# Hybrid diffusion step on one core: decayed keys before the last level's placement, turned keys read before the logarithm, three gate halves read in the next head's first level

## The chip, the cores and the metric

The kernel runs on one core of a Trainium2 chip. The metric is device time in microseconds (us) of one launch; the time before is the median of three runs. Engines are called as in the profile: PE is TensorE (PEld its weight loads), DVE VectorE, ACT ScalarE, POOL GpSimd, SP SyncE, which here only issues DMAs. Every engine runs its own instruction stream in the order in which it was written and waits on semaphores.

## What is computed

One trunk layer for 128 context tokens and 512 latent tokens (640 in all, width 1024): a mixer (a gated linear recurrence over four heads, called HGRN2, beside differential attention), then a mixture of 16 experts. The change lies in the recurrence alone:

```python
def hgrn2_scan(q, f, i, s0):              # f = forget gate, k = 1 - f, v = i, chunks of HG_CHUNK
    def step(S, inp):
        qc, lfc, kc, vc = inp             # lfc = log(f)
        b = jnp.cumsum(lfc, axis=2)
        inter = jnp.einsum('bhtd,bhde->bhte', qc * jnp.exp(b), S)
        rel = jnp.where(mask, b[:, :, :, None, :] - b[:, :, None, :, :], -jnp.inf)
        attn = jnp.einsum('bhtd,bhtsd,bhsd->bhts', qc, jnp.exp(rel), kc)
        o = inter + jnp.einsum('bhts,bhse->bhte', attn, vc)
        bL = b[:, :, -1]
        S = jnp.exp(bL)[..., None] * S + jnp.einsum('bhsd,bhse->bhde', kc * jnp.exp(bL[:, :, None] - b), vc)
        return S, o
# it runs forwards and backwards (own forget gates); o_f + o_b is RMS-normed per head and times silu(hg)
# the merge gates are g = sigmoid(h @ w_in[:, gate columns] + b_gate)
```

## The kernel before

One launch, all engines hand-scheduled: a list `STEPS` is written once, and each engine's program walks it and issues its own part of every step. So the place of a step in the list sets its place in the queue of every engine that has a part in it, and nothing else. PSUM is four pairs of banks; `use` books each write to a pair in the order of the list, `begin` makes PE wait until the pair's earlier contents were released, `filled` makes a reader wait for the writer.

Stages: norm and input projections (to about 204 us), attention with gate projections between (to 355), the recurrence of four heads (355 to 580), branch and output projections, router (to 740), experts (to the end). Projections in 32-bit are split into a high and a low part: three matmuls (lines 1750 to 1752) per tile, after ACT made the high part (`w_hi`, line 940) and DVE the low part (`w_lo`, line 1215).

A head `h` of the recurrence (the change is at its end and at the start of the next):

- **Levels** `("lev", h, 0..6)`: DVE subtracts (line 1299, always one level ahead), ACT takes two exponentials (line 1059), DVE makes two products (lines 1518, 1519), PE multiplies 20 small tiles (line 1953), DVE puts the scores of a level in their places (`place`: line 1307, for the last level 1311). Between the levels PE projects the next head's forget gates and queries (24 matmuls each).
- **`prep`**: ACT takes the exponentials `E[1]` (line 1069) and ten tiles of `exp(bL - b)` (line 1074, then `s_ebl2`), then copies the placed scores into `attn` (line 1078, then `s_attn`). DVE places level 5, then level 6, which waits for `s_attn`, then makes the **decayed keys** `Kb * E[0]` (line 1532), which PE waits for.
- **`kb`, `prep2`, `q`**: DVE makes the next head's `Kb` (1494) and `QB` (1538). ACT takes the next head's **logarithm** (line 1048, behind a table load of its own), DVE runs the two **scans** over it (1499, 1500). The scans stand ahead of `states` in DVE's queue.
- **`states`**: PE turns the decayed keys of both directions (line 1962), ACT reads them out of PSUM (**turned keys** `kTs`, the line 944 of 128x512), PE multiplies them with the values into `U` (1969), DVE reads `U` and carries the states `SC` (1547, 1553).
- **`qs`, `o`, `pre`, `diag`**: ACT's SiLU of the next queries (line 944, 128x640, with a table load); PE makes the head's output `o` (1979, 1984), which needs the last `SC`; DVE adds the keys (1506) and subtracts for level 0 (1299); PE makes the diagonal (1943), DVE reads it (1318).
- **Gate halves** `half(k, pair)`: 24 matmuls for half of a gate row; `drain(k)` is ACT's read of it (line 1098). Halves 25, 27 and 28 are made behind `states` of heads 0, 1, 2; half 26 behind `o` of head 0. SP stores them (line 792).
- **`sqr`**: ACT's square of `o` (1089), DVE's sum (1562), POOL's root (859, 860), DVE's two products (1568, 1571).

With heads 1 and 2 PE also makes a modulation row (`("mod", 7)`, `("mod", 8)`, 16 matmuls of line 1844) between the last level and the turns; ACT reads it behind the logarithm (`modr`).

Of the kernel before, what the change touches and what calls it, by code (L numbers as in the profile page):

```python
# [28 lines left out]
LEVELS = 7  # L29
# [10 lines left out]
def fused_step(nc, A, outs):  # L40
# [8 lines left out]
    with ExitStack() as ctx:  # L49
# [95 lines left out]
        kT = part(2560, 2560).rearrange("p (h t) -> p h t", h=H)  # L145
# [140 lines left out]
        STEPS = []  # L286
# [73 lines left out]
        def drain(k):  # L360
            STEPS.append(("glv", k // 2, k % 2))
# [29 lines left out]
        for h in range(H):  # L391
            todo = projections(h + 1) if h + 1 < H else []
            for lv in range(LEVELS):
                STEPS.append(("lev", h, lv))
                if (h, lv) in LEVEL_SPLITS:
                    split(*LEVEL_SPLITS[h, lv])
                if lv == 2 and h:
                    STEPS.append(("oTe", h - 1))
                if todo:
                    STEPS.append(todo.pop(0))  # L400
                if h + 1 < H and lv in (3, 5):
                    STEPS.append(("f", h + 1, lv // 2 - 1))
                if lv == 0:
                    if h == 0:
                        STEPS.append(("modr", 6))
                    if h == 1:
                        drain(26)
                    if h == 0:
                        STEPS.append(("modc", 6))
                    if h >= 2:  # L410
                        STEPS.append(("modv", 5 + h))
                    if h:
                        STEPS.append(("sqr", h - 1))
                if lv == 1 and h == 0:
                    STEPS.append(("modv", 6))
                if lv == 1 and h:
                    STEPS += [("sqg", h - 1), ("oT", h - 1)]
                if h == H - 1 and lv in (2, 4, 6):
                    drain(28 + lv // 2)
                if h == H - 1 and lv in (0, 2, 4):  # L420
                    half(29 + lv // 2, 1)
# [6 lines left out]
                STEPS.append(("kb", h + 1))  # L428
            STEPS.append(("prep2", h))
            if h + 1 < H:  # L430
                STEPS.append(("q", h + 1))
                if h == 0:
                    drain(24)
                else:
                    STEPS.append(("modr", 6 + h))
            else:
                STEPS.append(("hi", ("br", 1, 0)))
            STEPS.append(("states", h))
            if h + 1 < H:
                STEPS.append(("qs", h + 1))  # L440
                k = (25, 27, 28)[h]
                half(k, 3)
                drain(k)
            else:
                STEPS.append(("lo", ("br", 1, 0)))
                STEPS += [("ol", kt) for kt in range(4, 8)]
                STEPS.append(("hi", ("br", 0, 0)))
# [52 lines left out]
        for st in STEPS:  # L500
            k = st[0]
# [39 lines left out]
            elif k == "states":  # L541
                h = st[1]
# [95 lines left out]
        for key, _, _ in PIECES:  # L638
            k = key[0]
# [282 lines left out]
        def _(act):  # L922
# [38 lines left out]
            for n, st in enumerate(STEPS):  # L961
                k = st[0]
# [48 lines left out]
                elif k == "da":  # L1011
# [19 lines left out]
                    if n >= 2:  # L1031
                        h, i = ITER[n - 2]
                        oa_made(act, n - 2)
                        a.activation(oa[:, h, P * i:P * i + P], oaT, ACT.Copy, scale=subln8).then_inc(s_oa, 1)
                elif k == "f":
                    h, d = st[1], st[2]
# [8 lines left out]
                elif k == "q":  # L1045
                    h = st[1]
# [18 lines left out]
                elif k == "prep":  # L1065
# [11 lines left out]
                    for r in HALF:  # L1077
                        ins = a.activation(attn_c[r, :, r], within[r], ACT.Copy)
                    ins.then_inc(s_attn, 1)
                elif k == "states":  # L1080
                    h = st[1]
                    for d in range(2):
                        evac(kTs[:, d, 0:512], ("kT", h, d), src=bank(6 + d))
# [109 lines left out]
        def _(dve):  # L1193
# [10 lines left out]
            def own(sig):  # L1204
                count[sig.name] = count.get(sig.name, 0) + 1
                dve.wait_ge(sig, count[sig.name])
# [211 lines left out]
            for n, st in enumerate(STEPS):  # L1418
# [107 lines left out]
                elif k == "prep":  # L1526
                    h = st[1]

                    place(h, LEVELS - 2)
                    place(h, LEVELS - 1)  # L1530
                    dve.wait_ge(s_ebl2, h + 1)
                    v.tensor_tensor(E[0], Kb, E[0], ALU.mult).then_inc(s_ksb, 1)
                    own(s_ksb)
                elif k == "prep2":
                    h = st[1]
                    dve.wait_ge(s_eb, h + 1)
# [679 lines left out]
```

## Time and profile before

| | us |
|---|---|
| median of 3 runs (lowest, highest) | 1310.19 (1309.8, 1312.47) |
| the profiled execution | 1313.82 |
| its span, first to last instruction | 1312.0 |
| recurrence, four heads with the first one's projections | about 355 to 580 |
| of it the four head ends | about 404 to 424, 457 to 480, 512 to 532, 556 to 575 |

Busy shares over the whole span: PE 94%, DVE 76%, ACT 55%. A busy PE is not always a fast one: the granted clock has two levels in this trace, 1.00 (2.4 GHz) and 0.50 (1.2 GHz). Inside the recurrence PE waits in many short stretches, and each row of a timeline names in brackets how long the engine sat idle ahead of it and which instruction ended that. The rows of an engine's timeline stand in the order of its queue, so the row behind a waiting one waits with it.

### The profile page before, as it was taken

How to read it: one execution, taken by the hardware profiler on the slowest of the kernel's cores; microseconds unless marked ns; L12 is line 12 of the kernel's file. 1: busy time of each engine (PE TensorE's matmuls, PEld its weight loads, DVE VectorE, ACT ScalarE, POOL GpSimd, SP SyncE). 2: the span in 40 equal slices, each digit the busy share in tenths (PEclk: the TensorE clock that was granted, in tenths of full speed). 3: DMA queues.
4: the chain of work that ended last, by engine and by line, in shares of the span. 5: the costliest groups of instructions: out<-in, count | busy, mean ns of one | idle time of the engine just before them, and what ended most of it. 6: DMA issues, size and time to landing. Idle time of an engine off the chain costs nothing.

```text
span 1312.0 us, 18145 instructions
## 1 busy us (share of the span) xinstructions
PE 1235.7 (94%) x6817; PEld 915.1 (70%) x6817; DVE 995.6 (76%) x968; ACT 727.5 (55%) x769; POOL 341.1 (26%) x192
## 2 busy tenths in 40 slices
PE   7989999999998989779899899999999999999995
PEld 2667888888978876779776366666666666666663
DVE  3777425564267797878956889999999999999993
ACT  3322225555456758553312377777777777777771
POOL 1022001112000010100000002555656665555322
PEclk9989999999998989889998799999999999999998
DMA  8711521112331233044535499999999999999991
GB/s 311 260 54 53 191 78 55 56 48 66 98 108 48 70 92 127 25 172 172 194 142 204 158 402 401 393 392 385 391 384 390 383 388 385 390 383 390 394 361 31
DMA packets 111858, 296.06 MB, mean 226 GB/s; under 512 B 7092, under 2 KB 33076, under 8 KB 111800
## 3 DMA queue, kind: packets, MB, share of 16 engines
q1 hardware_dynamic: 108280, 284.25, 57.9%
q0 software_dynamic: 3520, 11.01, 3.6%
q8 instruction: 39, 0.64, 0.2%
q14 instruction: 19, 0.16, 0.0%
HBM read 278.47 MB, written 16.78 MB: 225 GB/s over the span
## 4 chain that ended last, share of the span: by engine, by line
PE 48%; DVE 2%; DMA 1%; ACT 1%; issue 0%; POOL 0%; DVEq 0%; ACTq 0%; POOLq 0%
PE ps L1750 15%; PE ps L1751 15%; PE ps L1752 15%; PE ps L1844 1%; PE ps L2071 1%; PE ps L2087 1%; DVE arena L1339 1%; PE ps L2033 0%; PE ps L2046 0%; DMA arena<-in_w_out_dram 0%; DMA arena<-xn_rows,arena 0%; ACT w_hi L940 0%; DVE arena L1594 0%; DVE arena L1590 0%; DVE w_lo L1215 0%
## 5 line engine op out<-in xcount | busy, mean ns | idle before, releaser
L1750 PE MATMUL ps<-w_hi,act_hi 128*80 128x512 f32 (+1 forms) x856 | 341.0, 398 | 10.1 <-DVE arena L1243 4.0
L1669 DVE TENSOR_TENSOR w_lo<-arena,w_hi 128x2048 fp32r<-128x2048 f32 x144 | 325.5, 2286 | 22.5 <-ACT w_hi L1169 17.6
L1751 PE MATMUL ps<-w_lo,act_hi 128*80 128x512 f32 (+1 forms) x856 | 337.5, 394 | 0.0
L1752 PE MATMUL ps<-w_hi,act_lo 128*80 128x512 f32 (+1 forms) x856 | 336.6, 393 | 0.0
L1169 ACT ACTIVATE w_hi<-arena 128x2048 fp32r<-128x2048 f32 x135 | 258.6, 1918 | 93.9 <-PE ps L1752 93.7
L1750 PE MATMUL ps<-act_hi,w_hi 128*128 128x320 f32 x576 | 185.3, 322 | 6.0 <-DVE w_lo L1215 3.0
L1750 PEld LDWEIGHTS ps<-w_hi,act_hi 128*80 128x80 f32 (+1 forms) x856 | 139.0, 162 | 71.8 <-DVE arena L1243 4.9
L1752 PEld LDWEIGHTS ps<-w_hi,act_lo 128*80 128x80 f32 (+1 forms) x856 | 138.9, 162 | 59.4 <-issue 0.7
L1751 PE MATMUL ps<-act_lo,w_hi 128*128 128x320 f32 x576 | 179.9, 312 | 0.0
L1752 PE MATMUL ps<-act_hi,w_lo 128*128 128x320 f32 x576 | 179.9, 312 | 0.0
L1751 PEld LDWEIGHTS ps<-w_lo,act_hi 128*80 128x80 f32 (+1 forms) x856 | 139.2, 163 | 55.4 <-issue 1.1
L859 POOL TENSOR_SCALAR arena<-arena 128x1 f32<-128x1 f32 (+2 forms) x44 | 13.8, 313 | 450.5 <-ACT arena L1025 190.3
L1750 PEld LDWEIGHTS ps<-act_hi,w_hi 128*128 128x128 f32 x576 | 110.3, 192 | 9.3 <-DVE w_lo L1215 3.6
L1215 DVE TENSOR_TENSOR w_lo<-arena,w_hi 128x2048 fp32r<-128x2048 f32 (+1 forms) x34 | 73.6, 2166 | 56.6 <-ACT w_hi L940 55.8
L1669 DVE TENSOR_TENSOR act_lo<-arena,act_hi 128x2048 fp32r<-128x2048 f32 x48 | 109.8, 2287 | 7.4 <-ACT act_hi L1169 6.1
L944 ACT ACTIVATE arena<-ps 128x512 f32<-128x512 f32 (+5 forms) x81 | 48.9, 616 | 117.3 <-PE ps L1844 32.2
L905 POOL DMA_INDIRECT out_dram<-arena x16 | 73.0, 4563 | 151.9 <-DVE arena L1695 151.9
L1751 PEld LDWEIGHTS ps<-act_lo,w_hi 128*128 128x128 f32 x576 | 110.2, 191 | 0.0
L1752 PEld LDWEIGHTS ps<-act_hi,w_lo 128*128 128x128 f32 x576 | 110.0, 191 | 0.0
L1169 ACT ACTIVATE act_hi<-arena 128x2048 fp32r<-128x2048 f32 x45 | 86.3, 1918 | 36.6 <-PE ps L1752 35.8
L940 ACT ACTIVATE w_hi<-arena 128x2048 fp32r<-128x2048 f32 (+1 forms) x34 | 61.5, 1810 | 54.8 <-PE ps L1752 25.9
L1844 PE MATMUL ps<-arena 128*2 128x512 f32 x144 | 71.5, 655 | 7.1 <-DMA arena<-in_w_mod_dram 7.1
(220 smaller groups left out, 1732.6 us busy)
## 6 DMA issues: line engine op xcount, KB each, us to landing
arena<-in_w_exp_gate_dram SPq DMA_DIRECT2D x64, 1024.0 KB, 8.5
arena<-in_w_exp_up_dram SPq DMA_DIRECT2D x64, 1024.0 KB, 7.0
arena<-in_w_exp_down_dram SPq DMA_DIRECT2D x64, 1024.0 KB, 7.9
arena<-in_w_mod_dram SPq DMA_DIRECT2D x23, 1024.0 KB, 5.2
arena<-in_w_in_dram SPq DMA_DIRECT2D x18, 1024.0 KB, 5.8
arena<-in_w_in_dram SPq DMA_DIRECT2D x12, 512.0 KB, 5.2
gl_raw<-arena SPq DMA_DIRECT2D x32, 160.0 KB, 1.8
arena<-gl_raw SPq DMA_DIRECT2D x8, 640.0 KB, 10.3
```

Of the source, the lines that this page charges most:

```text
L859: link(g.tensor_scalar(out, ss, 1.0 / n, EPS, ALU.mult, ALU.add))
L905: g.indirect_dma_start(out=y_sample[0], out_offset=bass.IndirectOffsetOnAxis(ap=iscat[0:CAP_LAT, 0:1], axis=0), in_=ye[0:CAP_LAT, :], in_o ...
L940: a.activation(hl(key)[0][:, 0:w], rawv(key)[:, 0:w], ACT.Copy).then_inc(s_hi, 1)
L944: release(a.activation(dst, src, func, **kw), key)
L1169: a.activation(EWh[j % NEW], eraw[(j + 2) % NRE], ACT.Copy).then_inc(s_eh, 1)
L1215: v.tensor_tensor(l_[:, 0:w], rawv(key)[:, 0:w], h_[:, 0:w].bitcast(F32), ALU.subtract).then_inc(s_lo, 1)
L1339: ins = v.scalar_tensor_tensor(out=out, in0=w[:, kk, :], scalar=by, in1=out, op0=ALU.mult, op1=ALU.add)
L1669: v.tensor_tensor(EWl[sl], eraw[slot], EWh[sl].bitcast(F32), ALU.subtract).then_inc(s_el, 1)
L1750: t.matmul(out, sh, mh, start=start, stop=False)
L1751: t.matmul(out, sh, ml, start=False, stop=False)
L1752: return t.matmul(out, sl, mh, start=False, stop=stop)
L1844: ins = t.matmul(bank(2 * modpair(j))[0:2, :], cond[:, kt, :], w[:, kk, :], start=kt == 0, stop=kt == 7)
```

## The change

Three moves and no new instruction:

1. In `prep` of every head DVE makes the decayed keys ahead of the placement of level 6. They wait for `s_ebl2` alone.
2. ACT's read of the turned keys becomes a step of its own, `("kT", h)`, ahead of the next head's logarithm in heads 0 to 2; in head 3 it stays behind the same weight split.
3. ACT's reads of gate halves 25, 27 and 28 go from behind their own matmuls into level 0 of the next head, behind its exponentials (and a weight split, where one stands there); that of half 26 goes behind the square of head 0's output.

```diff
@@ -401,16 +401,18 @@
                 if lv == 0:
+                    if h:
+                        drain((25, 27, 28)[h - 1])
                     if h == 0:
                         STEPS.append(("modr", 6))
-                    if h == 1:
-                        drain(26)
                     if h == 0:
                         STEPS.append(("modc", 6))
                     if h >= 2:
                         STEPS.append(("modv", 5 + h))
                     if h:
                         STEPS.append(("sqr", h - 1))
+                    if h == 1:
+                        drain(26)
@@ -428,19 +430,18 @@
             if h + 1 < H:
-                STEPS.append(("q", h + 1))
+                STEPS += [("kT", h), ("q", h + 1)]
                 if h == 0:
                     drain(24)
                 else:
                     STEPS.append(("modr", 6 + h))
             else:
-                STEPS.append(("hi", ("br", 1, 0)))
+                STEPS += [("hi", ("br", 1, 0)), ("kT", h)]
             STEPS.append(("states", h))
             if h + 1 < H:
                 STEPS.append(("qs", h + 1))
                 k = (25, 27, 28)[h]
                 half(k, 3)
-                drain(k)
@@ -1077,7 +1078,7 @@
-                elif k == "states":
+                elif k == "kT":
                     h = st[1]
                     for d in range(2):
                         evac(kTs[:, d, 0:512], ("kT", h, d), src=bank(6 + d))
@@ -1527,10 +1528,10 @@
                     place(h, LEVELS - 2)
-                    place(h, LEVELS - 1)
                     dve.wait_ge(s_ebl2, h + 1)
                     v.tensor_tensor(E[0], Kb, E[0], ALU.mult).then_inc(s_ksb, 1)
                     own(s_ksb)
+                    place(h, LEVELS - 1)
```

PE's, POOL's and SP's queues are the same instruction for instruction; only DVE's and ACT's differ.

ACT at the end of head 1, before. The 64x5x64 row is the last copy into `attn`, 1048 the logarithm with its table load, 2x512 the modulation row, 128x512 the turned keys, 128x640 the SiLU, 1098 the read of half 27, 1059 the next head's exponentials:

```order
L1078 ACTIVATE arena<-arena 64x5x64
L1048 ACT_TABLE_LOAD
L1048 ACTIVATE arena<-arena 128x1280 [waits s_f]
L944 ACTIVATE arena<-ps 2x512 [waits psum_full0]
L944 ACTIVATE arena<-ps 128x512 [waits psum_full3] x2
L944 ACT_TABLE_LOAD [waits psum_full1,s_qb]
L944 ACTIVATE arena<-ps 128x640
L1098 ACTIVATE arena<-ps,arena 128x320 [waits psum_full3,s_gst1]
L1059 ACT_TABLE_LOAD
L1059 ACTIVATE arena<-arena 128x2x5x64 [waits s_sub]
```

The same place in the changed kernel (its lines below the first edit are one or two higher):

```order
L1079 ACTIVATE arena<-arena 64x5x64
L945 ACTIVATE arena<-ps 128x512 [waits psum_full3] x2
L1049 ACT_TABLE_LOAD
L1049 ACTIVATE arena<-arena 128x1280 [waits s_f]
L945 ACTIVATE arena<-ps 2x512 [waits psum_full0]
L945 ACT_TABLE_LOAD [waits psum_full1,s_qb]
L945 ACTIVATE arena<-ps 128x640
L1060 ACT_TABLE_LOAD
L1060 ACTIVATE arena<-arena 128x2x5x64 [waits s_sub]
L1060 ACTIVATE arena<-arena 128x2x5x64
L941 ACTIVATE w_hi<-arena 128x2048 [waits psum_full3,s_raw1]
L1099 ACTIVATE arena<-ps,arena 128x320 [waits psum_full3,s_gst1]
```

The two reads that wait for PE's turns (`psum_full3`) now stand ahead of the logarithm and its table load, and the read of half 27 stands behind the exponentials and the split of a weight.

DVE at the same place, before: 1307 places level 5, 1311 level 6, 1532 is the decayed keys, 1494 the next `Kb`, 1538 `QB`, 1499 and 1500 the scans, 1547 the first read of `U`:

```order
L1307 COPY_PREDICATED arena<-arena,ps 128x320 [waits psum_full3,psum_free2]
L1311 COPY_PREDICATED arena<-arena,ps 64x5x64 [waits s_attn,psum_full2,psum_free3]
L1311 COPY_PREDICATED arena<-arena,ps 64x5x64
L1532 TENSOR_TENSOR arena<-arena 128x1280 [waits s_ebl2,psum_free2]
L1494 TENSOR_SCALAR arena<-arena 128x1280 [waits s_fa,s_ksb]
L1538 TENSOR_TENSOR arena<-arena 128x2x512 [waits s_st0,s_eb,s_f]
L1499 SCALAR_TENSOR_TENSOR arena<-arena 128x640 [waits s_ln,s_qb]
L1500 SCALAR_TENSOR_TENSOR arena<-arena 128x640 [waits s_v]
L1547 COPY arena<-ps 128x128 [waits psum_full2,s_st,s_scan]
```

And in the changed kernel:

```order
L1308 COPY_PREDICATED arena<-arena,ps 128x320 [waits psum_full3,psum_free2]
L1532 TENSOR_TENSOR arena<-arena 128x1280 [waits s_ebl2,psum_free3]
L1312 COPY_PREDICATED arena<-arena,ps 64x5x64 [waits s_attn,psum_full2,s_ksb]
L1312 COPY_PREDICATED arena<-arena,ps 64x5x64
L1495 TENSOR_SCALAR arena<-arena 128x1280 [waits s_fa,psum_free2]
L1539 TENSOR_TENSOR arena<-arena 128x2x512 [waits s_st0,s_eb,s_f]
L1500 SCALAR_TENSOR_TENSOR arena<-arena 128x640 [waits s_ln,s_qb]
L1501 SCALAR_TENSOR_TENSOR arena<-arena 128x640 [waits s_v]
L1548 COPY arena<-ps 128x128 [waits psum_full2,s_st,s_scan]
```

The decayed keys no longer wait for `s_attn`; the scans still wait for the logarithm (`s_ln`), and the reads of `U` still stand behind the scans.

ACT in level 0 of head 1, changed kernel: 1060 the exponentials of levels 0 and 1, 1099 the reads of halves 25 and 26, 1090 the square of head 0's output, which stood before in the order 25, exponentials, 26, square:

```order
L1060 ACTIVATE arena<-arena 128x2x5x64 [waits s_sub]
L1060 ACTIVATE arena<-arena 128x2x5x64
L1099 ACTIVATE arena<-ps,arena 128x320 [waits psum_full3,s_gst1]
L1090 ACTIVATE arena<-ps 128x640 [waits psum_full0,s_scan]
L1099 ACTIVATE arena<-ps,arena 128x320 [waits psum_full3,s_gst0]
L1060 ACTIVATE arena<-arena 128x2x10x32 [waits s_sub]
```

The exponentials of level 0 no longer stand behind half 25, and the square no longer behind half 26; those of level 1 stand behind half 26 as before.

## Rows read from the trace of the kernel before

**Rows 1.** ACT's timeline, end of head 0: start, length, instruction [idle before <-releaser].

```profile
419.79 0.53 ACT L1098 ACTIVATE arena<-ps,arena 128x320 f32<-128x320 f32 x1 [5.72 <-PE ps L1752]
```

**Rows 2.** DVE's timeline, end of head 0.

```profile
405.93 1.05 DVE L1311 COPY_PREDICATED arena<-arena,ps 64x320 f32<-64x320 uint8 x2 [1.71 <-ACT arena L1078]
...
410.77 1.49 DVE L1499 TENSOR_TENSOR_SCAN arena<-arena 128x640 f32<-128x640 f32 x1
...
423.09 0.82 DVE L1518 TENSOR_TENSOR arena<-arena 128x640 f32<-128x640 f32 x1 [2.17 <-ACT arena L1059]
```

**Rows 3.** PE's timeline, end of head 0 and level 1 of head 1.

```profile
411.71 3.75 PE L1969 MATMUL ps<-arena 128*128 128x128 f32 x16 [2.06 <-ACT arena L944]
...
419.51 0.61 PE L1979 MATMUL ps<-arena 128*128 128x128 f32 x4
...
432.48 0.74 PE L1953 MATMUL ps<-arena 128*64 128x64 f32 x18 [1.01 <-DVE arena L1519]
```

**Rows 4.** ACT's timeline, end of head 1.

```profile
462.43 1.27 ACT L1048 ACTIVATE arena<-arena 128x1280 f32<-128x1280 f32 x1 [2.28 <-DVE arena L1494]
464.61 1.61 ACT L944 ACTIVATE arena<-ps 2x512 f32<-2x512 f32 x3 [0.92 <-PE ps L1844]
466.24 1.28 ACT L944 ACT_TABLE_LOAD   x1
467.54 0.70 ACT L944 ACTIVATE arena<-ps 128x640 f32<-128x640 f32 x1
```

**Rows 5.** DVE's timeline, end of head 1 and level 0 of head 2.

```profile
463.80 1.49 DVE L1499 TENSOR_TENSOR_SCAN arena<-arena 128x640 f32<-128x640 f32 x1
...
467.14 0.29 DVE L1547 COPY arena<-ps 128x128 f32<-128x128 f32 x1 [0.33 <-PE ps L1969]
...
474.85 0.82 DVE L1518 TENSOR_TENSOR arena<-arena 128x640 f32<-128x640 f32 x1 [0.87 <-ACT arena L1059]
...
477.15 2.29 DVE L1215 TENSOR_TENSOR w_lo<-arena,w_hi 128x2048 fp32r<-128x2048 f32 x1
```

**Rows 6.** PE's timeline, end of head 1, levels 0 and 1 of head 2.

```profile
464.45 1.09 PE L1962 MATMUL ps<-arena 128*128 128x128 f32 x8
...
471.26 0.61 PE L1979 MATMUL ps<-arena 128*128 128x128 f32 x4
...
479.50 0.64 PE L1750 MATMUL ps<-act_hi,w_hi 128*128 128x320 f32 x1 [2.10 <-DVE w_lo L1215]
...
485.73 0.69 PE L1953 MATMUL ps<-arena 128*64 128x64 f32 x16
```

**Rows 7.** A stretch of 2 us: busy (x instructions) of PE, PEld, DVE, ACT, POOL, clock, DMA.

```profile
480.00:482.00 2.00, 2.00 (x9) 2.00 (x8) 1.93 (x3) 0.07 (x1) 1.49 (x1) 0.50 0.66 143
```

**Rows 8.** DVE's timeline, end of head 2 and level 0 of head 3.

```profile
518.15 1.49 DVE L1499 TENSOR_TENSOR_SCAN arena<-arena 128x640 f32<-128x640 f32 x1
...
522.01 0.29 DVE L1547 COPY arena<-ps 128x128 f32<-128x128 f32 x1 [0.83 <-PE ps L1969]
...
529.71 0.82 DVE L1518 TENSOR_TENSOR arena<-arena 128x640 f32<-128x640 f32 x1 [0.88 <-ACT arena L1059]
```

**Rows 9.** PE's timeline, end of head 2.

```profile
519.31 1.09 PE L1962 MATMUL ps<-arena 128*128 128x128 f32 x8
```

**Rows 10.** ACT's timeline, end of head 3.

```profile
555.84 3.02 ACT L1074 ACTIVATE arena<-arena 128x128 f32<-128x128 f32 x10
```

**Rows 11.** DVE's timeline, end of head 3.

```profile
559.83 1.04 DVE L1311 COPY_PREDICATED arena<-arena,ps 64x320 f32<-64x320 uint8 x2 [3.53 <-ACT arena L1078]
...
566.53 0.29 DVE L1547 COPY arena<-ps 128x128 f32<-128x128 f32 x1 [2.87 <-PE ps L1969]
```

**Rows 12.** PE's timeline, end of head 3.

```profile
562.45 1.97 PE L1962 MATMUL ps<-arena 128*128 128x128 f32 x8 [5.82 <-DVE arena L1532]
...
569.59 0.68 PE L1979 MATMUL ps<-arena 128*128 128x128 f32 x4 [1.94 <-DVE arena L1553]
...
573.65 0.71 PE L1984 MATMUL ps<-arena 128*128 128x128 f32 x4
```

## The prediction

> **What bounds the kernel now.** The views were read in this order: the page's busy shares and slices (PE 94% busy; the waits of PE lie in the recurrence, 404 to 580 us), then the timelines of ACT, DVE and PE around the four head ends, since every moved step stands there. What the reader is to see in them is which engine is late to whom.
>
> At the end of head 0 DVE idles 1.71 us until the copies into `attn` are done and only then makes the decayed keys [rows 2]; PE idles until it has them, and 2.06 us more until ACT has read the turned keys [rows 3]. ACT sits 5.72 us before gate half 25 [rows 1], and the next head's exponentials, which stand behind it, keep DVE idle for 2.17 us [rows 2].
>
> At the end of heads 1 and 2 it looks alike and is not. There PE is busy with a modulation row until it turns the keys, at 464.45 and 519.31, with no idle time ahead [rows 6, 9]. The decayed keys were ready long before. The logarithm and the scans run in that time: the logarithm from 462.43 [rows 4], the scans from 463.80 and 518.15 [rows 5, 8]. DVE then waits only 0.33 and 0.83 us for PE at its first read of `U`, and 0.87 and 0.88 us for the exponentials [rows 5, 8]. So DVE's chain is nearly as late as PE's: scans, states, keys, level 0.
>
> At the end of head 3 no logarithm follows. PE idles 5.82 us for the decayed keys [rows 12], DVE 3.53 us for `attn` ahead of them [rows 11].
>
> **The sum** is made against the profiled execution: 1313.82 us, of which 1312.0 are span. It lies 3.6 above the median of 1310.19, so I add the difference to the median.
>
> One length serves three places. From the start of the first scan to the first product of the next head's level 0, DVE needs 474.85 - 463.80 - 0.33 - 0.87 = 9.85 us of its own work [rows 5]; head 2 gives the same (529.71 - 518.15 - 0.83 - 0.88 = 9.85) [rows 8]. The two products take 1.75 more.
>
> **Heads 1 and 2: the turned keys ahead of the logarithm.** ACT now waits for PE's turns with the logarithm queued behind, and DVE's scans, `U` reads and all of level 0 behind that. Head 1: turns from 464.45, the first half is there about 0.6 later (half of 1.09, and one matmul's depth), ACT reads both by 466.2 (1.1 of the 1.61 for three reads), then the table load, 1.28, which used to lie in idle time and is now exposed, then the logarithm, 1.27 [rows 4, 6]. It ends at 468.8 and the scans start at 468.85 instead of 463.80. First product: 468.85 + 9.85 = 478.7 instead of 474.85, since the two old waits are swallowed. That is **3.85 late**. The same working for head 2, turns at 519.31: scans at 523.7, first product at 533.55 instead of 529.71, again **3.85 late** [rows 8, 9].
>
> What PE makes of it. `o` of head 1 could start at 471.26 [rows 6]; it needs the last `SC`, which DVE now has 4.6 later, about 474.85. PE idles 3.6 us. After idles of 2.06 and 2.10 us it ran slowly (16 matmuls in 3.75 us; 9 in 2 us at a granted clock of 0.50) [rows 3, 6, 7], so I take `o` at the slow clock, as in head 3: 569.59 to 574.36, 4.8 us [rows 12]. It ends at 479.65, the diagonal and the turned row at 480.8, just as the products are done (480.45). DVE reads the diagonal until 481.05 and makes the low part of the forget weights, 2.29 [rows 5]: PE's projection starts at 483.4, 3.9 after the old 479.50 [rows 6]. But the old one ran at the slow clock, 6.2 us until 485.73 [rows 6, 7]. The new one has only 1.8 us of idle time ahead and a busy stretch of 6.5 us before that; I take it at full clock, 3.8 us, to 487.2. DVE's level 1 products, 3.95 late, end at 487.75. PE's level 1 starts at 487.8: **+2.1** for head 1. From there each engine waits on the others in a ring (projection, sigmoid, exponentials, products), so nothing swallows it.
>
> Head 2 had no slow stretch there to give back, and head 3's level 0 is a chain of DVE, ACT and POOL that PE waits for: **+3.9**. Bounds for these two: 0.9 better at each if the logarithm were not late (the exponentials leave their place behind the gate half, 0.87 and 0.88), 4.6 worse at each if every delay of the scans reached PE.
>
> **Head 0.** No modulation row stands in PE's way. Decayed keys from 405.0, when ACT's ten exponentials end (0.97 before it could place level 6), ready at 406.5; PE turns them at 407.0, when its projection ends. ACT reads them until 408.75, load and logarithm until 411.35, scans from 411.45: 0.7 late against 410.77 [rows 2]. First product of head 1: 411.45 + 9.85 = 421.3 instead of 423.09, **1.8 early**, since the exponentials no longer wait for half 25 [rows 1, 2]. PE makes `U` and half 25 by 414, then idles 3.4 us for `SC` (417.45 instead of the old start of `o` at 419.51 [rows 3]), pays the slow clock, 4.8 instead of 3.0, and ends `o` where it did before. Half 26, level 0 and a projection follow back to back as before, until 431.4. Level 1's products are then ready (the square is no longer behind half 26), where PE waited 1.01 us [rows 3]: **-1.1**. Bound: if the clock stays up, `o` ends 1.8 earlier, the half 26 waits for ACT's read of half 25 until 421.8, and level 1 starts at 430.0, -2.4.
>
> **Head 3.** The decayed keys start when the ten exponentials end, 555.84 + 3.02 = 558.86, instead of 560.90 behind `attn` and the placement [rows 10, 11]. PE, ACT, `U` and DVE's reads (waiting 2.87 us for PE [rows 11]) all follow 2.0 earlier; the weight split on ACT ends at 561.63, in time. **-2.0**. SP's gate loads start when this head's `o` is done, so the branch stage shifts as a whole.
>
> **No cost:** the level 6 placement (1.05) goes between the decayed keys and `Kb`; DVE reaches the scans before the logarithm is done. The late reads of halves 27 and 28 free pair 3 for level 1, which comes 6 us later, and SP's stores behind them come ahead of loads that wait longer for other slots.
>
> Sum: -1.1 + 2.1 + 3.9 - 2.0 = **+2.9 us**, 1313.1.
>
> Of a table switch the rows show 1.28 us, and the next instruction 0.02 us behind it (466.24 + 1.28, then 467.54) [rows 4]. The Trainium skill (ScalarE: Activation LUTs, What ACT_TABLE_LOAD costs) adds a drain of 1.38 us to each switch, 2.66 in all; the load newly exposed in heads 1 and 2 would then cost 2.8 more together, 1315.9. The trace doesn't show that drain, so the sum does not have it.
>
> **Rivals.**
> - *The clock falls once more* in the 1.8 us before head 2's first projection. For: 2.06 and 2.10 us of idle time made PE slow [rows 3, 6]. Against: 1.8 is less, and behind a long busy stretch. It would run 2.5 us slower; 0.6 of that is hidden under DVE: +4.9, 1315.1.
> - *Head 0 gives its bound*, the clock staying up: +1.6, 1311.8. Against: 3.4 us is more than any wait that left the clock up.
> - *Faster:* the scans' delay does not decide, as if ACT could serve the logarithm in time; then only waits vanish: -2.4, -0.9, -0.9, -2.0 = -6.2, 1304.0. It decides only where the logarithm ends within about 1.2 us (0.33 + 0.87) of its old time; the rows give 5.05. For it: my 0.6 for the turns and the exposed load are read from one execution each. That the reads still stand where they stood is ruled out by the order.
>
> **Chances.** Forecast 42%, clock falls once more 27%, head 0's bound 17%, faster 9%, larger losses 5%. The forecast's own spread is about 1.3 either way (1311.8 to 1314.4). About 0.2%, 2.6 us, is what a measurement of this kernel can tell from no change; the forecast lies just above it, so it feeds two chances: slower 57%, within 0.2% 33%, faster 10%. The range leaves out most of the faster case and the largest losses: 1310.0 to 1316.4.
>
> **What would show it.** In the changed profile: ACT's logarithm behind its two reads, ending near 468.8 less head 0's 1.1; DVE's scans 4 to 5 us later at heads 1 and 2; a PE wait of about 3.5 us before `o` in heads 0, 1 and 2, with a clock of 0.50 behind it; head 3's wait for decayed keys down from 5.82 to 3.8. Wrong would make it: `o` of heads 1 and 2 without a wait, or a clock that stays at 1.00 through them.

## The result and the profile after

| | before | changed |
|---|---|---|
| median of 7 runs each (lowest to highest), us | 1310.19 (1309.65 to 1312.47) | 1316.24 (1315.05 to 1317.28) |
| profiled execution, us | 1313.82 | 1316.05 |
| its span, us | 1312.0 | 1314.3 |

The ratio of times is 1.0038 with a 95% interval of 1.0029 to 1.0048: the change costs 5.0 us (3.8 to 6.3), 0.4%. The forecast was 1313.1, with a sum of +2.9. The sign and the steps on ACT and DVE were right, two terms were too small. The median of 1316.24 lies only 0.2 us inside the upper end of the range (1316.4) and outside the forecast's own spread (1311.8 to 1314.4).

The whole span says little here (2.3 us), since the profiled execution of before lies 3.6 us above its median, and the changed kernel is already 1.5 us ahead of it before the first moved step. So I read stretches between fixed points of PE's stream: **A** from the last level of head 0 to the turns of head 1, **B** from there to the turns of head 2, **C** from there to level 5 of head 3 (its last but one), **D** from there to the turn of head 3's output. Each holds one head end. The changed kernel and all those below start A 0.3 to 2.3 us earlier than the kernel before does (401.12 against 402.65 for the change); nothing moved lies ahead of A, and this is in none of the sums. Most of it goes with PE's clock in the input stage. From 20 to 30 us the kernel before had 0.89 and the changed one 1.00 (columns as in [rows 7]):

```profile
20.00:30.00 10.00, 8.50 (x36) 3.37 (x35) 5.50 (x9) 4.58 (x6) 1.48 (x4) 0.89 0.93 344
...
20.00:30.00 10.00, 8.27 (x38) 3.40 (x37) 5.55 (x8) 4.57 (x6) 1.48 (x4) 1.00 0.93 345
```

Of the thirteen profiled executions of this document, the four with 0.86 to 0.89 there begin A at 402.30 to 402.65, the nine with 1.00 at 400.37 to 401.47.

| us | A | B | C | D | sum |
|---|---|---|---|---|---|
| before | 61.80 | 54.86 | 34.78 | 25.36 | |
| forecast of the difference | -1.1 | +2.1 | +3.9 | -2.0 | +2.9 |
| changed | 60.16 | 57.84 | 39.68 | 23.41 | |
| measured difference | -1.64 | +2.98 | +4.90 | -1.95 | +4.3 |

The +4.3 lies inside the interval of the paired runs.

**Head 1.** ACT's timeline of the changed kernel (start, length, instruction, idle before). It answers to [rows 4]:

```profile
461.98 1.09 ACT L945 ACTIVATE arena<-ps 128x512 f32<-128x512 f32 x2 [6.84 <-PE ps L1963]
463.08 1.28 ACT L1049 ACT_TABLE_LOAD   x1
464.37 1.27 ACT L1049 ACTIVATE arena<-arena 128x1280 f32<-128x1280 f32 x1
...
475.40 1.89 ACT L941 ACTIVATE w_hi<-arena 128x2048 fp32r<-128x2048 f32 x1
477.20 0.51 ACT L1099 ACTIVATE arena<-ps,arena 128x320 f32<-128x320 f32 x1
```

ACT idles 6.84 us until PE has turned the keys, and only then come the table load and the logarithm. DVE's timeline, to be held against [rows 5]:

```profile
465.75 1.49 DVE L1500 TENSOR_TENSOR_SCAN arena<-arena 128x640 f32<-128x640 f32 x1 [6.67 <-ACT arena L1049]
...
475.65 0.82 DVE L1519 TENSOR_TENSOR arena<-arena 128x640 f32<-128x640 f32 x1
...
477.95 2.29 DVE L1216 TENSOR_TENSOR w_lo<-arena,w_hi 128x2048 fp32r<-128x2048 f32 x1
```

The scans wait 6.67 us for the logarithm. PE turned the keys at 461.28 (first row below), so the scans start 4.47 us and the first product 14.37 us behind the turns. In the kernel before the product stood 474.85 - 464.45 = 10.40 behind them [rows 5, 6]: 3.97 late. PE's timeline, for [rows 6]:

```profile
461.28 1.09 PE L1963 MATMUL ps<-arena 128*128 128x128 f32 x8
...
471.86 0.68 PE L1980 MATMUL ps<-arena 128*128 128x128 f32 x4 [3.60 <-DVE arena L1554]
...
474.93 0.80 PE L1944 MATMUL ps<-arena 128*64 128x64 f32 x20
477.76 0.41 PE L1763 MATMUL ps<-arena 2*128 2x2 f32 x4 [2.03 <-ACT arena L1099]
478.10 0.80 PE L1954 MATMUL ps<-arena 128*64 128x64 f32 x20
480.30 0.64 PE L1751 MATMUL ps<-act_hi,w_hi 128*128 128x320 f32 x1 [1.40 <-DVE w_lo L1216]
...
485.54 0.80 PE L1954 MATMUL ps<-arena 128*64 128x64 f32 x20
```

Two things are to be seen. PE waits 3.60 us before `o` (471.86), as forecast, and yet `o` takes only 3.07 us. And there is a wait that I did not have: 2.03 us before the turned modulation row (line 1763), ended by ACT's read of gate half 27 at 477.20. Two stretches (columns as in [rows 7]; the second is head 2's `o`):

```profile
480.00:482.00 2.00, 1.70 (x6) 1.70 (x7) 1.93 (x4) 0.31 (x1) 0.72 (x1) 0.57 0.32 38
...
529.70:532.00 2.30, 2.30 (x11) 2.30 (x12) 2.23 (x3) 0.03 (x1) 0.00 (x0) 0.50 0.18 57
```

In head 1 the projection behind the waits begins at a clock of 0.57, in head 2 `o` runs at 0.50. Head 1's `o`, behind the same wait of 3.60 us, ran at 1.00.

**Head 2.** PE's timeline, then DVE's:

```profile
519.12 1.09 PE L1963 MATMUL ps<-arena 128*128 128x128 f32 x8
...
529.70 1.19 PE L1980 MATMUL ps<-arena 128*128 128x128 f32 x4 [3.60 <-DVE arena L1554]
...
535.24 0.80 PE L1944 MATMUL ps<-arena 128*64 128x64 f32 x20
...
541.30 0.80 PE L1954 MATMUL ps<-arena 128*64 128x64 f32 x20 [0.48 <-DVE arena L1520]
```

```profile
533.50 0.83 DVE L1519 TENSOR_TENSOR arena<-arena 128x640 f32<-128x640 f32 x1
...
536.19 0.49 DVE L1319 TENSOR_TENSOR arena<-ps,arena 128x320 f32<-128x320 f32 x1 [1.01 <-PE ps L1944]
```

The same wait of 3.60 us, and here `o` takes 5.54 us at the lower clock. The diagonal is late, and DVE, which was already 3.97 late (533.50 is 14.38 behind the turns at 519.12), loses 1.01 us more.

**Heads 0 and 3.** Head 0, PE and DVE, for [rows 3] and [rows 2]:

```profile
405.47 1.03 PE L1963 MATMUL ps<-arena 128*128 128x128 f32 x8
...
416.00 1.19 PE L1980 MATMUL ps<-arena 128*128 128x128 f32 x4 [3.61 <-DVE arena L1554]
...
420.42 0.80 PE L1944 MATMUL ps<-arena 128*64 128x64 f32 x20
```

```profile
409.88 1.49 DVE L1500 TENSOR_TENSOR_SCAN arena<-arena 128x640 f32<-128x640 f32 x1 [1.69 <-ACT arena L1049]
...
419.80 0.83 DVE L1519 TENSOR_TENSOR arena<-arena 128x640 f32<-128x640 f32 x1
```

Head 3, PE's turns, for [rows 12], where the same row had 5.82:

```profile
565.22 1.97 PE L1963 MATMUL ps<-arena 128*128 128x128 f32 x8 [3.88 <-DVE arena L1532]
```

### The profile page after: what moved, and what is told of

The parts are those of the page before. It is cut to its first block, busy times and chain, and to the rows that moved or that the text cites. A ratio compares the mean times of both kernels' runs of the same rounds, so it can differ in the third digit from the quotient of the medians.

```text
span 1314.3 us, 18145 instructions
## 1 busy us (share of the span) xinstructions
PE 1233.8 (94%) x6817; PEld 915.6 (70%) x6817; DVE 995.6 (76%) x968; ACT 727.4 (55%) x769; POOL 341.0 (26%) x192
## 4 chain that ended last, share of the span: by engine, by line
PE 48%; DVE 2%; DMA 1%; ACT 1%; issue 0%; POOL 0%; DVEq 0%; ACTq 0%; POOLq 0%
PE ps L1751 15%; PE ps L1752 15%; PE ps L1753 15%; PE ps L1845 1%; PE ps L2072 1%; PE ps L2088 1%; DVE arena L1340 1%; PE ps L2034 0%; PE ps L2047 0%; DMA arena<-in_w_out_dram 0%; DMA arena<-xn_rows,arena 0%; ACT w_hi L941 0%; DVE arena L1595 0%; DVE arena L1591 0%; DVE w_lo L1216 0%
## 5 line engine op out<-in xcount | busy, mean ns | idle before, releaser
L901 POOL COPY arena<-arena 64x1 uint32 (+1 forms) x16 | 88.2, 5512 | 13.3 <-DMA out_dram<-arena 13.3
```

The lines of the kernel that those rows point to most:

```text
L901: g.tensor_copy(iscat[0:CAP_LAT, 0:1], iS[0:CAP_LAT, bass.ds(e, 1)]).then_inc(s_icq, 1)
```

## The experiments

The theory: in heads 1 and 2 the logarithm, put behind ACT's reads of the turned keys, delays DVE's scans and all that is queued behind them; the two other moves are gains that this swallows. The rivals: the loss comes from the late reads of the gate halves, which hold a PSUM pair longer; or from the clock, which falls in the new wait before `o`. Differences in the table below are to before, in us; "sum" is over the stretches A to D of one profiled execution each, "by runs" is the ratio with its interval, times the median of before (1310.2 to 1312.4, depending on the runs it was compared with). Where the two differ by a us or two, the ratio counts: each sum rests on one execution, and all are taken against the same execution of before, which was itself slow in places (head 1's projection above all, see p_keys).

| kernel | A | B | C | D | sum | by runs |
|---|---|---|---|---|---|---|
| changed | -1.64 | +2.98 | +4.90 | -1.95 | +4.3 | +5.0 (3.8 to 6.3) |
| p_turned | +1.31 | +3.00 | +5.14 | +0.12 | +9.6 | +7.6 (5.9 to 9.3) |
| p_drains | -1.01 | -1.84 | -0.84 | -0.08 | -3.8 | -5.6 (-7.3 to -3.9) |
| p_keys | -3.28 | -0.98 | -0.01 | -2.36 | -6.6 | -4.6 (-6.3 to -2.8) |
| p_head0 | -0.41 | -0.61 | -0.84 | -1.94 | -3.8 | -6.3 (-8.4 to -4.2) |
| q_keysdrains | -1.54 | -2.89 | -0.82 | -2.02 | -7.3 | -7.7 (-9.4 to -5.9) |
| q_scanslate | -2.70 | +2.40 | +2.22 | -1.94 | 0.0 | +0.1 (-1.0 to +1.4) |
| q_filler | -2.62 | +3.43 | +3.98 | -1.95 | +2.8 | +3.4 (2.1 to 4.9) |
| q_drainsplit | -0.15 | +1.95 | +4.07 | -1.94 | +3.9 | +4.6 (2.9 to 6.2) |
| r_fill | -4.10 | -1.96 | -0.84 | -0.94 | -7.8 | -6.7 (-8.5 to -5.0) |
| r_split | -1.56 | -1.83 | -0.85 | -1.95 | -6.2 | -6.2 (-7.9 to -4.3) |
| r_both | -4.11 | -2.09 | -0.84 | -0.99 | -8.0 | -6.6 (-8.4 to -4.7) |

### One part alone

p_turned: the kernel before with only the turned keys read ahead of the logarithm.

```diff
-                STEPS.append(("q", h + 1))
+                STEPS += [("kT", h), ("q", h + 1)]
...
-                elif k == "states":
+                elif k == "kT":
```

> Of the change only the move of ACT's read of the turned keys ahead of the next head's logarithm; the decayed keys and the gate halves stay as before. Theory (the logarithm and the scans behind the turned keys are the loss): heads 1 and 2 lose 3.9 us each at the first product of the next head, part of it hidden in PE's stream, head 0 stays within 0.5, head 3 unchanged: 6 to 8 us slower than before, and the whole loss of the change and more. Rival A (the gate halves held back cost the time): within 1 us of before. Rival B (the slow clock behind PE's wait for the states is the loss, whoever causes the wait): as the theory, but with no more than 2 us of it outside the stretches of clock 0.50.

p_drains: only the late reads of the gate halves.

```diff
                 if lv == 0:
+                    if h:
+                        drain((25, 27, 28)[h - 1])
...
                 half(k, 3)
-                drain(k)
```

> Of the change only the later reads of the gate halves. Theory: the next head's exponentials come 2.2, 0.9 and 0.9 us earlier; PE gains about 1 in head 0 and 0.9 in heads 1 and 2: 2 to 3 us faster than before. Rival A (the gate halves held back cost the time, since the turned modulation row waits for the pair that half 27 holds): 3 us slower or more.

p_keys: only the decayed keys ahead of the last placement.

```diff
                     place(h, LEVELS - 2)
-                    place(h, LEVELS - 1)
                     dve.wait_ge(s_ebl2, h + 1)
...
                     own(s_ksb)
+                    place(h, LEVELS - 1)
```

> Of the change only the decayed keys ahead of the last placement. Theory: head 3 gains 2.0, head 0 0.9 (the logarithm waits for the next keys, which come 0.9 earlier), heads 1 and 2 nothing, since PE is busy with the modulation row: 2.5 to 3 us faster. Rival A says nothing of it. Rival B (clock): head 3 gains more than 2, since its slow stretch is shorter.

Measured: one part alone costs 7.6 us (a ratio of 1.0058, 1.0045 to 1.0071), the two others each gain (0.9957, 0.9944 to 0.9970; and 0.9965, 0.9952 to 0.9979). p_turned carries +3.0 and +5.1 in heads 1 and 2, as the whole change does (+3.0 and +4.9). In head 0, where no more than 0.5 was expected, it loses 1.31: a new wait of 1.98 us stands before `o`, and `o` behind it took 4.66 us instead of 2.99. So the first rival falls: the late reads alone do not lose anything, they gain 5.6. Both gains were larger than expected. p_drains gave 1.84 in head 1 where 0.9 was the wait for the exponentials, because the projection behind it was shorter as well (5.24 instead of 6.23 us). p_keys gave 3.28 in head 0. There PE waits 2.80 us before `U`, in one piece instead of in two (1.39 and 2.06), and in this execution the clock stayed up behind it:

```profile
408.76 2.02 PE L1969 MATMUL ps<-arena 128*128 128x128 f32 x16 [2.80 <-ACT arena L944]
```

The profiled execution of p_keys, 1304.35, is the fastest of its six (median 1307.80), so its -6.6 says more than the kernel usually gives. Its -0.98 in head 1 is no gain of the move, of which nothing was expected there. The projection starts 15.05 us behind the turns in both kernels, but took 5.25 us here and 6.23 in the profiled execution of before. So before was slow at this place, and about 1 us of every B in the table is that slow stretch and not the edit. Against p_keys, whose head 1 has the same waits, the change loses 57.84 - 53.88 = 3.96 us there.

### The change without the turned keys, and with them in head 0 alone

q_keysdrains is p_drains and p_keys together, that is the change without ("kT", h); p_head0 is the change with ("kT", h) ahead of the logarithm in head 0 alone.

```diff
-                STEPS += [("kT", h), ("q", h + 1)]
+                if h in (0,):
+                    STEPS.append(("kT", h))
+                STEPS.append(("q", h + 1))
...
+            if h not in (0,):
+                STEPS.append(("kT", h))
             STEPS.append(("states", h))
```

> The change, but in heads 1 and 2 the turned keys are read behind the logarithm and the modulation row, as before. Theory: the two losses go and 0.9 is won in each, head 0 and head 3 keep their 1.6 and 1.9: 5.3 us faster than before, 9 to 11 faster than the change. Rival A (gate halves): still 1 us or more slower than before. Rival B (clock): the waits of 3.6 us ahead of the outputs of heads 1 and 2 are gone and with them the slow stretches, as the theory.

> The change without its middle part: decayed keys first and gate halves late, but the turned keys read behind the logarithm in every head. Theory (the logarithm behind the turned keys is the whole loss): the gains of the two parts add, about 1 (gate halves) and 3 (keys) in head 0, 1.8 in head 1, 0.8 in head 2, 2.3 in head 3: 8 to 9.5 us faster than before. Rival (the two gains are one and the same wait counted twice): no more than 5.5 faster, as either part alone.

Measured: 1306.79 for p_head0 (0.9952, 0.9936 to 0.9968) and 1305.02 for q_keysdrains (0.9941, 0.9928 to 0.9955). Both beat both kernels. For q_keysdrains 8 to 9.5 had been expected; 7.7 (5.9 to 9.4) is a little less. From q_keysdrains to the changed kernel the stretches differ by -0.10, +5.87, +5.72 and +0.07: in these executions the move of the turned keys costs 5.8 us in each of heads 1 and 2, and nothing in heads 0 and 3. For head 0 that is because each of the two has a slow stretch of its own there (`U` 3.75 us in q_keysdrains, `o` 4.42 in the change). Where neither has one, in r_fill and q_filler below, A is 57.70 without the move and 59.18 with it: it costs 1.5 us there too. PE's rows of q_keysdrains in head 1 show what the 5.87 is made of:

```profile
474.22 0.41 PE L1763 MATMUL ps<-arena 2*128 2x2 f32 x4 [1.06 <-ACT arena L1099]
...
476.77 0.42 PE L1751 MATMUL ps<-act_hi,w_hi 128*128 128x320 f32 x1 [1.40 <-DVE w_lo L1216]
...
480.94 0.80 PE L1954 MATMUL ps<-arena 128*64 128x64 f32 x20 [0.40 <-DVE arena L1520]
```

The turns of this kernel are at 462.56, so the projection starts 14.21 us behind them, against 19.02 in the changed kernel: 4.81, which is the 3.97 of the scans and the 0.84 that the freed exponentials had given and that is swallowed. The other 1.07 is the length of the projection with what follows, 4.17 here and 5.24 there. In head 2 the same 4.8 and 0.9 for `o` at the lower clock make the 5.72 (q_filler, below, has head 2 without the slow `o`, at 4.80).

### The scans behind the states

q_scanslate is the change, but the scans stand behind DVE's reads of `U` and not ahead of them.

```diff
             if h + 1 < H:
+                STEPS.append(("scan", h + 1))
                 STEPS.append(("qs", h + 1))
...
-                elif k == "q":
+                elif k == "scan" or k == "q" and st[1] == 0:
```

> The change, with DVE's two scans moved behind its reads of U and its states, so that only the next head's level 0 waits for the logarithm and no longer the states. Theory: PE's waits of 3.6 us ahead of the outputs of heads 0, 1 and 2 go to 0; the first product of the next head stands 12.3 us after the turns of heads 1 and 2 (before 10.4, with the change 14.4): heads 1 and 2 together lose 2 to 4 us against before instead of 7.9, so 4 to 6 us faster than the change. Rival (the loss is ACT's own, its exposed table load and logarithm in front of the exponentials): the first product stays at 14.4 and the time within 1 us of the change.

DVE's timeline in head 1, where PE turns the keys at 460.55:

```profile
463.25 0.29 DVE L1549 COPY arena<-ps 128x128 f32<-128x128 f32 x1 [4.90 <-PE ps L1971]
...
466.20 1.49 DVE L1501 TENSOR_TENSOR_SCAN arena<-arena 128x640 f32<-128x640 f32 x1
...
473.16 0.83 DVE L1520 TENSOR_TENSOR arena<-arena 128x640 f32<-128x640 f32 x1
```

Measured: 1311.97, no different from before (1.0001, 0.9992 to 1.0011), 5 us better than the change. All three waits before `o` are gone. The states fill the time in which DVE waited for the logarithm, and the first product stands 12.61 us behind the turns, between the 10.40 of before and the 14.37 of the change. So the loss is the place of the scans in DVE's queue together with the late logarithm, as the theory has it: the same table load and the same logarithm on ACT at the same place, with other work ahead of the scans, cost 2.2 instead of 4.0. What is left of the loss in B and C (+2.40, +2.22) is that product, 2.21 late. One wait in head 1 even grew, that before the turned modulation row:

```profile
475.27 0.58 PE L1764 MATMUL ps<-arena 2*128 2x2 f32 x4 [4.11 <-ACT arena L1100]
```

It did not cost time by itself: the projection behind it starts 2.21 us later than before, as the product does.

### Products in the wait before `o`

q_filler puts 12 products of the identity with itself, whose results nobody reads, ahead of `o` of heads 0 to 2.

```diff
+                    if h + 1 < H:
+                        for _ in range(12):
+                            t.matmul(bank(6)[:, 0:P], ident, ident, start=True, stop=True)
                     begin(pe, ("o", h))
```

> The change, with 12 matmuls of the identity with itself (results unused, into a free half of pair 3) ahead of the output of heads 0, 1 and 2, so that PE works through about 3.0 of the 3.6 us that it waits there. Clock theory: the outputs of heads 0 and 2, 4.4 and 5.5 us long with the change, take 3.0; head 2 gets 1 us shorter, head 0 up to 1.4: 2 to 3 us faster than the change. Rival (the clock costs nothing, DVE's chain decides): within 0.5 us of the change.

PE in head 1 (each of the twelve counts as two rows, x24):

```profile
466.80 2.84 PE L1977 MATMUL ps<-arena 128*128 128x128 f32 x24
470.57 0.68 PE L1983 MATMUL ps<-arena 128*128 128x128 f32 x4 [0.93 <-DVE arena L1554]
...
473.64 0.80 PE L1944 MATMUL ps<-arena 128*64 128x64 f32 x20
476.48 0.55 PE L1763 MATMUL ps<-arena 2*128 2x2 f32 x4 [2.04 <-ACT arena L1099]
```

Measured: 1315.09 (1.0026, 1.0016 to 1.0037), about 1.5 us less than the change, where 2 to 3 were expected; the two intervals overlap. In the trace the waits before `o` are down to 0.92 or 0.93 and `o` takes 3.07 us in all three heads; without the products it took that in one of nine cases (they are listed at the end). Head 0 gains 0.98 by that and head 2 gains 0.92, down to +3.98, which is DVE's lateness and nothing else. Head 1, whose `o` had not been slow, gains nothing and is even 0.45 longer: the 2.04 before the turned row stands, and the projection runs slowly behind it (5.67 us to level 1). So the clock is a second, smaller part: about 0.9 us in head 2. The second rival does not carry the loss.

### The half's read ahead of the weight split

q_drainsplit is the change, but ACT reads the gate half straight behind the first exponentials of the level, ahead of the split `w_hi`.

```diff
                 STEPS.append(("lev", h, lv))
+                if lv == 0 and h:
+                    drain((25, 27, 28)[h - 1])
                 if (h, lv) in LEVEL_SPLITS:
...
                 if lv == 0:
-                    if h:
-                        drain((25, 27, 28)[h - 1])
```

> The change, with ACT's read of gate halves 25, 27 and 28 ahead of the weight split of level 0 instead of behind it (differs in head 2's level 0 alone). Theory: the turned modulation row, which shares the bank of half 27, no longer waits 2.03 us, PE's projection behind it runs at full clock, and the stretch from the turns of head 1 to those of head 2 is 0.9 us shorter than with the change, 56.9 instead of 57.8; the split comes 0.5 later and must not be late. Rival (the wait is hidden, since the projection waits for the split weights anyway, and the clock falls all the same): 57.8 or 0.5 more.

PE and ACT in head 1 (turns at 463.96):

```profile
474.55 1.19 PE L1980 MATMUL ps<-arena 128*128 128x128 f32 x4 [3.61 <-DVE arena L1554]
...
479.19 0.80 PE L1944 MATMUL ps<-arena 128*64 128x64 f32 x20
480.25 0.80 PE L1954 MATMUL ps<-arena 128*64 128x64 f32 x20
483.01 0.41 PE L1751 MATMUL ps<-act_hi,w_hi 128*128 128x320 f32 x1 [1.95 <-DVE w_lo L1216]
```

```profile
478.08 0.51 ACT L1099 ACTIVATE arena<-ps,arena 128x320 f32<-128x320 f32 x1
478.50 1.90 ACT L941 ACTIVATE w_hi<-arena 128x2048 fp32r<-128x2048 f32 x1
```

Measured: the wait before the turned row is gone and B is 56.81, +1.95 where the change has +2.98. This `o` took 4.64 us, close to the 4.8 of the forecast, the projection stood behind 1.95 us of waiting (the forecast: 1.8) and ran at the full clock (4.18 us to level 1). That is the course that the forecast drew for head 1, and it gives the +2.1 of the forecast. The kernel as a whole, 1316.86 (1.0035, 1.0022 to 1.0047), is not told apart from the change. In the profiled execution `o` of head 0 took 5.81 us instead of 4.42 and gave the gain back; whether that holds for the others is not shown.

### Versions without the turned keys

r_fill is q_keysdrains with ten such idle products between the turns and `U` of head 0; r_split is q_keysdrains with the half's read ahead of the split; r_both has both.

```diff
+                    if h == 0:
+                        for _ in range(10):
+                            t.matmul(bank(5)[:, 0:P], ident, ident, start=True, stop=True)
                     for d in range(2):
```

> Decayed keys first and gate halves late, turned keys behind the logarithm as before; besides, 10 matmuls of the identity with itself (results unused, into a bank that U writes next) between the turns and U of head 0, where PE waits 2.8 us for ACT. Clock theory: U and gate half 25 always run at full clock, 5.4 us from U to the output instead of 8.2; the stretch from the last level of head 0 to the turns of head 1 is 57.5 us instead of 60.3 (before 61.8): 9 to 10 us faster than before. Rival (the clock is not the cause of the 8.2 us, DVE's chain is): 60 us, and about 7.5 faster.

> Decayed keys first and gate halves late, turned keys behind the logarithm, and the gate halves read ahead of the weight split of level 0. Theory: the turned modulation row of head 1 no longer waits the 1.06 us, but PE had slack there; within 0.5 us of the kernel with the split first, 7 to 8 us faster than before. Rival (this wait costs as it did in the changed kernel): 1 us faster than that.

> Both: the 10 matmuls in head 0 and the gate halves ahead of the split. Theory: 9 to 10 us faster than before, as with the matmuls alone. Rival: 7.5.

Head 0 of q_keysdrains, then of r_fill:

```profile
410.50 3.75 PE L1970 MATMUL ps<-arena 128*128 128x128 f32 x16 [2.81 <-ACT arena L945]
```

```profile
406.22 2.40 PE L1968 MATMUL ps<-arena 128*128 128x128 f32 x20
409.21 2.02 PE L1973 MATMUL ps<-arena 128*128 128x128 f32 x16 [0.59 <-ACT arena L945]
```

Measured: 1303.96 (0.9949, 0.9935 to 0.9962), 1305.67 (0.9953, 0.9940 to 0.9967) and 1303.68 (0.9950, 0.9936 to 0.9964). All are 6 to 7 us faster than before, and not told apart from each other or from q_keysdrains by these runs. For r_fill and r_both 9 to 10 had been expected, so by the whole time that expectation missed. In the trace the idle products do what they should: `U` takes 2.02 us instead of 3.75 and A falls by 2.56. One execution alone would not show that, since `U` took 2.02 in p_keys as well, behind the same wait without any product in it; but r_both has 2.02 too, and r_split, without the products, 3.75. But D is 1.08 longer than in q_keysdrains at places that nothing touched, and B 0.93 (the projection of head 1, 5.11 us instead of 4.17). In D it is the projection behind the same wait, first q_keysdrains, then r_fill:

```profile
567.60 0.42 PE L1751 MATMUL ps<-act_hi,w_hi 128*128 128x320 f32 x1 [2.41 <-DVE act_lo L1577]
```

```profile
564.84 0.64 PE L1751 MATMUL ps<-act_hi,w_hi 128*128 128x320 f32 x1 [2.41 <-DVE act_lo L1577]
```

0.42 and 0.64 for the same first matmul behind the same 2.41 us: one execution had the upper clock in the 3 us from there (1.00) and the other the lower (0.50). r_split saves nothing. Its wait of 1.06 us before the turned row is gone, but PE then waits 2.11 instead of 1.40 us for `w_lo` and its projection starts 14.21 us behind the turns (462.60), exactly as in q_keysdrains:

```profile
476.81 0.42 PE L1751 MATMUL ps<-act_hi,w_hi 128*128 128x320 f32 x1 [2.11 <-DVE w_lo L1216]
...
482.05 0.80 PE L1954 MATMUL ps<-arena 128*64 128x64 f32 x20
```

That its B is 1.06 longer (-1.83 against -2.89) is the length of this projection, 5.24 us instead of 4.17, and not the moved read. q_keysdrains is the only one of these kernels whose projection took 4.17; p_drains, with the same waits, took 5.24 as well.

## Why the prediction was right or wrong

- **The length of DVE's work** (9.85 us from the first scan to the first product): right. 475.65 - 465.75 = 9.90 in head 1, 9.92 in heads 0 and 2.
- **The late logarithm** of heads 1 and 2: right. The scans were forecast 4.40 us behind the turns and came 4.47 behind them; the product was forecast 3.85 late and came 3.97 late. That the load lies exposed at 1.28 us and no more is seen too: it starts at 463.08, and the logarithm at 464.37. The drain of 1.38 us that the Trainium skill (ScalarE: Activation LUTs, What ACT_TABLE_LOAD costs) adds to each switch is not in this trace. That the 1315.9 with this drain comes so near to the time measured is luck.
- **The wait before `o`**: right, 3.60 to 3.61 us in three heads, where 3.4 to 3.6 was forecast.
- **`o` at the slow clock, 4.8 us**: this term was mis-sized, both ways. It took 4.42, 3.07 and 5.54 us behind the same wait. The price came from the one slow `o` that the trace of before had [rows 12], and a clock that may come back within the stretch or stay up has no one price. The argument against head 0's bound, that 3.4 us is more than any wait that left the clock up, was wrong too: head 1's `o` ran at 1.00 behind 3.60 us.
- **Head 2, +3.9**: +4.90. The term was the product's 3.85 alone. I had taken `o` to end under cover of DVE's work, which it does at 4.8 us and does not at 5.54: DVE waited 1.01 us for the diagonal. q_filler, with `o` at 3.07, gives +3.98. The loss passes even the bound of 4.6, which was the delay of the last `SC` (the forecast's own rows give 5.05 - 0.33 = 4.72), since that bound left the clock out.
- **Head 1, +2.1**: +2.98. Two steps failed, and only the second cost time. The first is "the late reads of halves 27 and 28 free pair 3 for level 1, which comes 6 us later". Level 1 is not the first user of pair 3: the turned modulation row is, before level 0. It waited 2.03 us for half 27's read, which stood behind exponentials and a split of 1.89 us. The wait itself cost nothing; the projection had to wait for `w_lo` anyway, and started 3.97 late where 3.9 was forecast. The second is "I take it at full clock": the clock was at 0.57 behind the two waits (2.03 and 1.40), and the projection and what follows took 5.24 us, where I had taken 4.4. That is the whole 0.9. With that read moved (q_drainsplit) head 1 costs +1.95. q_drainsplit also had a slow `o` where the change had a fast one, so it does not single out the wait as what brought the clock down; that is argued from the order of the rows. Against it stand p_keys and r_split, where that wait is 0 and the projection took 5.25 and 5.24 us all the same, though behind 2.10 and 2.11 us; so what brought the clock down stays open.
- **Head 0, -1.1**: -1.64. Turns 1.56 early as forecast; scans 4.41 behind the turns (forecast 4.45). The half us more is `o` at 4.42 instead of 4.8 and some rounding of its end. In the sum it hid half a us of what heads 1 and 2 lost beyond the forecast. The bound of -2.4 is what q_filler's head 0 shows (-2.62), where the clock stayed up.
- **Head 3, -2.0**: -1.95, with the wait at 3.88 (forecast 3.8).
- **The rivals.** "Faster, 1304.0" is what the kernel gives without the late logarithm: its terms -2.4, -0.9, -0.9 and -2.0 stand against -1.54, -2.89, -0.82 and -2.02 in q_keysdrains (of the -2.89, 2.06 is the length of the projection, 4.17 us against 6.23). That the scans' delay would not decide is refuted by p_turned and q_scanslate. "The clock falls once more", 1315.1, is nearest to the time measured, and came in part: the projection that it names ran slowly at its start, but for 0.9 us of loss and not 2.0, and the rest of the miss is the slower `o` of the next head.

What stays open is what decides the clock behind a given wait.

## What to carry to other kernels

A read that waits for another engine, put ahead of a table load and a function on an in-order engine, turns both from hidden into exposed: here 3.97 us on each of two heads, where DVE's own waits had shown 1.2 us of slack. Before moving a read later, list every user of the buffer it frees in program order, small ones too, since the first of them waits and not the one that you thought of (here it waited 2.03 us, hidden behind another wait). And take a bundle of moves apart: two of these three together gained 7.7 us, and the third turned that into a loss of 5.

## What was not expected of the hardware

The clock behind a wait did not follow from the length of the wait. Behind 3.60 or 3.61 us of idle time `o`, the same matmuls each time, took 3.07, 4.42, 4.64, 4.70, 5.54, 5.65, 5.70, 5.78 and 5.81 us in the changed kernel, p_turned (heads 1 and 2), p_head0 (head 0) and q_drainsplit. Behind 2.80 and 2.81 us `U` took 2.02 us in one execution and 3.75 in another. The projection of head 1 with what follows, behind 1.40 us each time, took 4.17, 5.11, 5.24 and 6.46 us, and behind 1.95 us 4.18 twice. A stretch of 3 us at either level therefore has a price of up to 2.7 us either way that one trace does not fix, and a comparison that rests on less than that needs the median of several runs or a stretch in which no such wait lies.
